# One output-weight chunk loaded early, experts and combine in one block, the inverses' transpose moved: a two-layer trunk on one core

## What is computed

```python
for layer in range(2):
    mix = hybrid_mixer(h, ...) if layer == 0 else rglru_mixer(h, ...)   # both end in @ w_out
    h = layer_norm(DN_ALPHA * h + mix, ln_g[layer, 0], ln_b[layer, 0])
    ffn = hierarchical_moe(h, ...)          # top group, then top 2 of its 8 experts
    h = layer_norm(DN_ALPHA * h + ffn, ln_g[layer, 1], ln_b[layer, 1])

# in hybrid_mixer, per chunk and head
t_inv = triangular_solve(eye + lower, eye, lower=True, unit_diagonal=True)
# in hierarchical_moe, per block of 128 rows of one expert
hid = silu(xi @ w_gate[e]) * (xi @ w_up[e]); yb = hid @ w_down[e]
y = segment_sum(yb * row_w[:, None], row_tok)
```

## Time and profile before

| | us |
|---|---|
| median of three runs | 2292.05 |
| lowest, highest | 2288.58, 2295.93 |
| the profiled execution's own time | 2292.08 |
| its span | 2290.3 |

### The profile page before, as it was taken

The page is one execution under the profiler, slowest core; times in us unless marked ns, Lnnn a source line. Parts: engine busy times, 40 slices in busy tenths (PEclk is TensorE's granted clock), DMA queues, the critical chain, the costliest instruction groups (busy, mean ns, idle before and its releaser), DMA issues. The chain is left out here.

```text
span 2290.3 us, 30226 instructions
## 1 busy us (share of the span) xinstructions
PE 2137.8 (93%) x10785; PEld 1741.7 (76%) x10785; DVE 1746.2 (76%) x1785; ACT 1409.3 (62%) x1509; POOL 499.4 (22%) x325
## 2 busy tenths in 40 slices
PE   8999966989999999999997999999899999999985
PEld 7777755878688888888883777768688888888862
DVE  5378866563799899889985785564799888988867
ACT  3344445253278877888775438753377888788852
POOL 0000040001223333333320001111133333333322
PEclk9999978999899999999998899999899999999997
DMA  4121011140199999999974231060299999999955
GB/s 157 47 66 45 28 30 56 25 196 38 43 359 391 381 385 386 399 387 393 386 267 174 89 114 37 19 241 37 99 365 395 381 384 397 383 397 385 391 199 239
DMA packets 133823, 526.12 MB, mean 230 GB/s; under 512 B 36816, under 2 KB 41328, under 8 KB 99952
## 3 DMA queue, kind: packets, MB, share of 16 engines
q1 hardware_dynamic: 114736, 491.46, 56.6%
q0 software_dynamic: 19008, 33.60, 3.9%
HBM read 505.32 MB, written 51.92 MB: 243 GB/s over the span
## 5 line engine op out<-in xcount | busy, mean ns | idle before, releaser
L2284 DVE TENSOR_TENSOR w_lo_e<-raw,w_hi_e 128x2048 fp32r<-128x2048 f32 x192 | 439.3, 2293 | 55.3 <-ACT w_hi_e L2236 50.3
L2236 ACT ACTIVATE w_hi_e<-raw 128x2048 fp32r<-128x2048 f32 x192 | 367.7, 1918 | 127.4 <-PE ps L1481 103.8
L1479 PE MATMUL ps<-w_hi_e,x_hi_e 128*128 128x512 f32 x1024 | 407.8, 398 | 6.0 <-DVE x_lo_e L2289 5.3
L1481 PE MATMUL ps<-w_hi_e,x_lo_e 128*128 128x512 f32 x1024 | 401.1, 392 | 0.0
L1480 PE MATMUL ps<-w_lo_e,x_hi_e 128*128 128x512 f32 x1024 | 400.9, 391 | 0.0
L2284 DVE TENSOR_TENSOR w_lo_e<-raw_more_e,w_hi_e 128x2048 fp32r<-128x2048 f32 x128 | 292.9, 2288 | 49.5 <-ACT w_hi_e L2236 49.4
L2236 ACT ACTIVATE w_hi_e<-raw_more_e 128x2048 fp32r<-128x2048 f32 x128 | 245.7, 1919 | 17.7 <-PE ps L1481 14.9
L2144 POOL DMA_INDIRECT expert_rows<-hT,idx_e x64 | 98.1, 1533 | 669.3 <-ACT hT L2250 669.3
L1479 PEld LDWEIGHTS ps<-w_hi_e,x_hi_e 128*128 128x128 f32 x1024 | 193.6, 189 | 45.4 <-DVE x_lo_e L2289 5.7
L1481 PEld LDWEIGHTS ps<-w_hi_e,x_lo_e 128*128 128x128 f32 x1024 | 193.4, 189 | 41.5
L1480 PEld LDWEIGHTS ps<-w_lo_e,x_hi_e 128*128 128x128 f32 x1024 | 193.8, 189 | 38.0
(11 more groups left out here) (441 smaller groups left out, 4337.6 us busy)
## 6 DMA issues: line engine op xcount, KB each, us to landing
raw<-in_moe_w_up SPq DMA_DIRECT2D x126, 1024.0 KB, 7.8
raw_more_e<-in_moe_w_down SPq DMA_DIRECT2D x64, 1024.0 KB, 7.7
raw_more_e<-in_moe_w_gate SPq DMA_DIRECT2D x62, 1024.0 KB, 7.1
hT<-in_moe_w_gate SPq DMA_DIRECT2D x62, 1024.0 KB, 7.0
raw<-in_moe_w_down SPq DMA_DIRECT2D x62, 1024.0 KB, 8.9
y_c<-expert_rows SPq DMA_DIRECT2D x32, 512.0 KB, 11.0
h_rows<-h SPq DMA_DIRECT2D x24, 512.0 KB, 3.4
w_ch<-in_w_ch SPq DMA_DIRECT2D x17, 512.0 KB, 3.6
```

Source lines behind the costliest of these rows:

```text
L1479: pe.matmul(out, lhs[0], rhs[0], start=start, stop=False)
L1481: return pe.matmul(out, lhs[1], rhs[0], start=False, stop=stop)
L2236: act.activation(w_hi[:, p.split, :], ring[p.raw], ACT.Copy).then_inc(taken, 1)
L2284: v.tensor_tensor(w_lo[:, p.split, :], ring[p.raw], w_hi[:, p.split, :].bitcast(F32), ALU.subtract).then_inc(split, 1)
```

## The change

It has three parts.

1. `inverse.turn` goes, in ScalarE's loop over attention's tiles, from behind `copy_share(6)` to ahead of `exps(7)`.
2. `combine` has no block of its own any more. It returns five functions that `expert_blocks` calls at the end of each engine's queue, in its own block. In the place of the barrier stand a semaphore `rows_there`, which GpSimd raises after its last wait for the scatters and SyncE waits for before the first load of y_c, and TensorE's wait for the last split of gathered rows. TensorE's idle matmuls go from 2 on PSUM bank 7 to 6 on bank 5. The tile y_c now lies over tiles of the experts.
3. In layer 1, chunk 6 of w_out is loaded in the recurrent block, when its weight buffer is free, and SyncE waits for it at the end of that block. `mix_and_route` loads the other seven, takes chunk 6 first, and has the order y0, w0, y1, w1. TensorE's idle matmuls at its start go from 5 to 3. The tiles of w_out and of the recurrent weights have fixed places for this.

```diff
+        at_out = at_end - 4 * KC * D
+        w_last = tuple(nc.alloc_sbuf_tensor_at(x, [P, KC, D], dt, offset=at_out) for x, dt in (("w_out_last", F32), ("w_out_last_r", F32R)))
+        place = at_end - 4 * 2 * KC * P
+        w_ch = tuple(nc.alloc_sbuf_tensor_at(x, [P, 2, KC, P], dt, offset=place) for x, dt in (("rw_ch", F32), ("rw_ch_r", F32R)))
...
-                    recurrent(m, gate, gate_r, w_ch)
+                recurrent(m, gate, gate_r, w_ch, w_last[0][:, EARLY_CHUNK, :])
...
-                expert_blocks(m, layer, raw, landed, route)
-            if layer == 0:
-                w_ch = sb_both("rw_ch", [P, 2, KC, P], scope=first)
-            combine(m, layer, out if layer == 1 else None, w_ch[0])
+                expert_blocks(m, layer, raw, landed, route, out if layer == 1 else None, w_ch[0])
...
@@ attention, scalar
                 for t in range(NT + 1):
+                    if t == NT - 1:
+                        inverse.turn(act)
                     if t < NT:
                         exps(t)
                     if t:
                         copy_p(t - 1)
                         copy_share(t - 1)
-                    if t == NT - 1:
-                        inverse.turn(act)
@@ recurrent, sync
+                sp.wait_ge(proj, N - 1)
+                sp.dma_start(w_early, a["w_out"][1][:, EARLY_CHUNK, :]).then_inc(s_early, 16)
+                sp.wait_ge(s_early, 16)
@@ mix_and_route
-        there = KC // 2 if half_there else 0
+        chunk = [EARLY_CHUNK] + [c for c in range(KC) if c != EARLY_CHUNK] if layer else list(range(KC))
+        there = 1 if layer else KC // 2
...
-        order = [("y", 0), ("y", 1), ("w", 0), ("w", 1), ("y", 2), ("w", 2), ("w", 3), ("y", 3),
+        order = [("y", 0), ("w", 0), ("y", 1), ("w", 1), ("y", 2), ("w", 2), ("w", 3), ("y", 3),
...
-                    sp.dma_start(w_out[:, n, :], a["w_out"][layer][:, n, :]).then_inc(s_w[n], 16)
+                    sp.dma_start(w_out[:, chunk[n], :], a["w_out"][layer][:, chunk[n], :]).then_inc(s_w[n], 16)
...
-                idle(m, pe, 7, 2 if half_there else 5)
+                idle(m, pe, 7, 3 if layer else 2)
@@ expert_blocks: sync, gpsimd, tensor, scalar, vector
+                transfer(sp)
...
+                pool.sem_inc(rows_there, 1)
+                add_shift(pool)
...
+                pe.wait_ge(x_split, 2 * r + 3)
+                mix_and_turn(pe)
...
+                root_and_evict(act)
...
+                normalise(v)
@@ combine
+    def transfer(sp):
+        sp.wait_ge(rows_there, 1)
         rows = m.y_dram.rearrange("(k t p) d -> t k p d", k=2, p=P)
...
-                idle(m, pe, 7, 2)
+        idle(m, pe, 5, 6)
```

More of the change, by code:

```diff
@@ L2030, in expert_blocks @@
     with scope:
+        with ExitStack() as passing:
+            y_c = sb(n_("y_c"), [P, NT, 2, D], scope=passing)
         more = sb(n_("raw_more"), [P, RAW - EARLY - 1, PIECE], scope=scope)
@@ new lines, in combine, with add_shift @@
+    gained, ready, last_ready, turned, copied, high_out, stored, s_dve = (sem(n_(x)) for x in
+        ("gained", "ready", "last_ready", "turned", "ht_out", "high_out", "stored", "dve"))
+    LAST = NT - 1
+    span = lambda t: slice(t * P, (t + 1) * P)
+    half = lambda hf: slice(hf * HALF, (hf + 1) * HALF)
+    def add_shift(pool):
+        if last:
+            pool.wait_ge(s_ln, 16)
+            for t in range(LAST):
+                pool.wait_ge(gained, t + 1)
+                pool.tensor_tensor(h[:, t, :], h[:, t, :], ln[:, 1, :], ALU.add).then_inc(ready, 1)
@@ new lines, in mix_and_turn, with mix, turn @@
+    def mix_and_turn(pe):
+        def mix(t):
+            pe.wait_ge(spread, t + 1)
+            for hf in range(2):
+                if t >= 2:
+                    pe.wait_ge(summed, 2 * (t - 2) + hf + 1)
+                for k in range(2):
+                    if hf == 0:
+                        pe.wait_ge(s_y[t][k], 16)
+                    mm = pe.matmul(ps[:, 2 * (t % 2) + hf, :], diag[:, t, k, :], y[:, t, k, half(hf)],
+                                   start=(k == 0), stop=(k == 1))
+                mm.then_inc(mixed, 1)
+        def turn(t):
+            pe.wait_ge(normed, t + 1)
+            if t == LAST:
+                pe.wait_ge(high_normed, 1)
+            if t >= 2:
+                pe.wait_ge(copied, t - 1)
+            for c in range(KC):
+                mm = pe.transpose(ps[:, 4 + 2 * (t % 2) + c // 4, (c % 4) * P:(c % 4 + 1) * P], h[:, t, c::KC], m.c(C_ID))
+            mm.then_inc(turned, 1)
+        idle(m, pe, 5, 6)
+        for t in range(NT):
+            mix(t)
+            if t >= 2 and not last:
+                turn(t - 2)
+        if not last:
+            turn(LAST - 1)
+            turn(LAST)
```

279 lines of the change are left out of this document (118 added, 161 removed).

## The result

The changed kernel takes **2276.28 us** (median of six executions, 2274.72 to 2277.67), the kernel before 2294.32 in the same comparison (2288.58 to 2298.59): ratio 0.993, 95% interval 0.9912 to 0.9949, so 12 to 20 us less. The forecast was 2276.2. Run once more as an experiment the changed kernel took 2278.6, ratio 0.9937 (0.9923 to 0.995).

What follows compares the result with a forecast made beforehand. TensorE, busy 93% of the span, was taken to lose time at joints between stages where one other queue works alone. Terms -4.5 - 11.3 + 1.1 - 1.2 = -15.9 took 2292.05 to 2276.2 us, range 2271.5 to 2284.

Steps and rivals of the forecast that it cites:

- part 1, attention: End of attention: transposes, their store and the 16 loads run earlier, SyncE ending at 389.85 for 394.33; -4.5 us.
- delta rule's clock: Start of the delta rule's stage: a shorter TensorE gap might change the half-clock stretch; between -1.2 and +1.0, taken as 0.
- part 2, first load of y_c, per layer: Experts to combine: SyncE's first load follows GpSimd's wait without its drain; -5.65 us per layer, -11.3 together.
- clock in the combine, layer 0: Start of layer 0's combine: a short fall to half clock after a 3.7 us TensorE gap; costs 0.8 us.
- clock in the combine, layer 1: Start of layer 1's combine: short clock fall mostly covered by TensorE's wait for tile 1's rows; costs 0.3 us.
- part 3 at the stage's end: Layer 1's projection: VectorE's 1.23 us wait is filled, later splits come 1.2 us earlier; -1.2 us in the sum.
- attention's last VectorE instruction ends at 387.04 + 2.0: End of attention: VectorE's tail moves 2.0 us later to 389.1, still 0.8 us before SyncE ends.
- The drain is over 5.5 us after that load at the latest.: Layer 1's combine: GpSimd's drain ends within 5.5 us of the first load, before its first addition some 9 us after.
- with half of the fall inside the gap: Layer 0's combine: half the clock's fall passes while TensorE is idle, so it costs 0.8 us in place of 2.3.
- long fall: Rival, both combines: half clock lasts 10 us from about the first product; +5.5 in place of +1.1, 2280.6 us; chance 0.14.
- The first product later than 6.5 us after the first load: Sign against the prediction, in the combine: a first product that late after the first load of y_c would prove it wrong.
- Another stage has changed its length by over 1 us: Sign against the prediction: any stage outside the change differing by over 1 us would prove it wrong.

Runs made afterwards that it cites:

- idle10: Changed kernel with ten idle matmuls in place of six ahead of each combine; 2275.64 us.
- gains_second: Changed kernel with ten idle matmuls ahead of each combine and layer 1's gains and shifts loaded behind tile 1's rows; 2271.4 us, ratio 0.9904.
- all_three: Changed kernel with ten idle matmuls, the gains behind tile 1's rows, and rank(0) moved two chunks into the last tile's products; 2270.44 us, ratio 0.9901.
- three_late_chunk: all_three with part 3 undone (no early chunk, order y0, y1, w0, w1, five idle matmuls); 2272.64 us, ratio 0.9917.
- after: The changed kernel itself, in its first measurement and profile, against the kernel before; 2276.28 us, ratio 0.993.
- after_again: The changed kernel run once more with no edit; 2278.6 us, ratio 0.9937.
- halves: Changed kernel with the two 512 KB loads of tile 0's rows split by columns into four of 256 KB, low halves first; 2281.43 us.
- turn_back: Changed kernel with only part 1 undone, the transposes behind tile 6's copies again; 2280.39 us, ratio 0.9949.
- late_chunk: Changed kernel with only part 3 undone: all eight chunks loaded at layer 1's projection, order y0, y1, w0, w1, five idle matmuls; 2275.61 us, ratio 0.9921.
- rank_apart: Changed kernel with rank(0)'s narrow matmuls moved two chunks into the last tile's products, in both layers; 2277.14 us.
- drain_first: Changed kernel with a GpSimd drain added between its last scatter wait and the raise of rows_there, each expert stage; 2287.24 us, ratio 0.9978.

## Why the prediction was right, point by point

The time was right to 0.1 us, which is partly luck. The forecast was 15.9 us less than 2292.05; the kernel before, measured again beside the changed one, took 2294.32, and the medians differ by 18.0. The terms measured in the first pair of profiles add up to -18.2 (-4.21 - 5.87 + 0.88 - 1.21 - 5.88 - 1.94) where the sum had -15.9, and scatter in the rest gives 0.8 back.

| term | forecast | measured |
|---|---|---|
| part 1, attention | -4.5 | -4.2 |
| delta rule's clock | 0 | -1.4 in one profile, scatter of 4.4 |
| part 2, first load of y_c, per layer | -5.65 | -5.9 |
| clock in the combine, layer 0 | +0.8 | +0.9; over the five kernels with six idle matmuls, whole loads and no added drain +0.9 to +2.4 |
| clock in the combine, layer 1 | +0.3 | -1.9; -0.8 to -1.9 |
| part 3 at the first addition | -1.2 | -1.2 |
| part 3 at the stage's end | -1.2 | +0.1 to -0.3 |

**Part 1.** The step "attention's last VectorE instruction ends at 387.04 + 2.0" was short by 1.2. The 2.0 of the moved instruction were right. But TensorE now pauses 3.3 us while ScalarE has the transposes and tile 7's exponentials, and its clock is down from 381.8 to 385.2, when the tail comes. Timeline of TensorE, turning the exponentials of tiles 6 and 7, in the changed kernel:

```profile
376.09 1.09 PE L626 MATMUL ps<-cst,scores 128*128 128x128 f32 x8
...
383.12 1.97 PE L626 MATMUL ps<-cst,scores 128*128 128x128 f32 x8
```

and before:

```profile
382.92 1.09 PE L627 MATMUL ps<-cst,scores 128*128 128x128 f32 x8
```

Tile 7's eight take 1.97 us in place of 1.09. So the margin of 0.8 us became -0.5, and the term 4.2 in place of 4.5. The profiles of idle10 and gains_second, whose code is the same here, bear the cause out: no stretch at half clock begins there, tile 7's eight take 1.09 us, and attention's last VectorE operation ends 58.6 and 58.7 us after the barrier in place of 60.1, ahead of SyncE, as forecast.

**Part 2.** The reading of the queue was right in both its halves, that the raise does not wait for the drain and that the drain alone was the hold: the first load stands 0.02 us behind the wait, and a drain put ahead of the raise costs 5.5 us again. The Trainium skill's rule on increments and drains (PSUM — Partial Sum Buffer, Engine vs sequencer instructions) agrees with both rows. One sentence failed: "The drain is over 5.5 us after that load at the latest." In layer 1 the drain stands behind GpSimd's last addition, 42 us after that load, and is what the closing barrier waits for last. In the eleven profiles with the joined block and no added drain that barrier opens 0.37 us behind SyncE's drain, in the other three 0.16. So the forecast left out 0.2 us, and whoever shortens the stores at the kernel's end will meet GpSimd's drain first.

**The clock in the combine.** The sign was wrong in layer 1, and with it that of the whole term: +1.1 forecast, -1.1 measured. Two steps failed. First, "with half of the fall inside the gap": in the changed kernel hardly any of it was, 0.2 us of 3.4 in layer 0 and 0.4 in layer 1. In the six profiles with six idle matmuls, one block and no drain, the fall in layer 0 begins 2.9 to 4.4 us after the first load, from 0.9 us ahead of the first product to 0.7 behind it. In layer 0 the profiles then fall into three groups:

| stretch at half clock, layer 0 | kernels | combine, us |
|---|---|---|
| none | gains_second, all_three, three_late_chunk, idle10 | 47.8, 47.8, 47.8, 48.5 |
| 3.4 us | after, after_again, halves | 49.1, 49.2, 49.2 |
| 6.8 us, from 2.9 to 3.0 on | turn_back, late_chunk, rank_apart | 50.4, 50.5, 50.5 |

Against the three at 47.8 the fall costs 1.3 to 1.5 or 2.6 to 2.8 us, and which of the two differs between executions. Why idle10 takes 0.7 more without a fall, from tile 1 on, no run says. The second group is the forecast's, the third lies toward the rival "long fall", to which I gave 0.14; it was there in three of six. Second, for layer 1 I compared only tile 0. The earlier trace rows show that TensorE waits 2.07 us for tile 1's rows, and I counted that as cover. I did not see that the wait itself lets the clock fall a second time: the record behind it takes 4.12 us for five matmuls, 0.82 each, which is the half-clock figure that I had used for tile 0. With the wait gone (gains_second, all_three, three_late_chunk) this fall is gone; yet the wait of 2.46 us in halves had none. The change took it away by making tile 0 slower. The advice in the Trainium skill against idle gaps (TensorE: Matmul & The Clock Gate, Why this matters for your kernels) was right about the mechanism in layer 0, where filling the gap takes the fall away; in layer 1 filling that gap alone made the combine longer, since another gap came behind it.

**Part 3.** Right at the place where it was derived, the first addition, and wrong in carrying it to the sum. "The later splits come 1.2 us earlier" holds through to the last addition; the stage's end does not follow, in both pairs of kernels.

**The signs that I named.** The first load behind the wait by under 0.5 us, the order of the transposes, and no idle time ahead of the first chunk: all there. Of the signs against, two were there as well. "The first product later than 6.5 us after the first load" came true with 7.29, and was badly put, since my own term of 0.8 implies 6.9. "Another stage has changed its length by over 1 us" came true for four (the first projection -2.1, the delta rule -1.4, layer 1's routing +1.9, and its experts up to the end of GpSimd's wait +1.6); this was scatter, and I had no measure of it from one profile. Layer 1's projection and routing shows how it arises. In the eleven profiles with rank(0) in its old place it takes 140.7 to 140.8 us four times, 143.6 to 143.8 five times, and 142.4 and 143.0 once each. In the first group a stretch at half clock of 3.4 us begins 105.6 to 105.8 us after the barrier; in the second one of 6.8 us at 105.3 to 105.4 (105.7 in late_chunk, where all of it is 1.2 later), and 3.4 us more at half clock follow before the stage ends (from 125.8 or 125.9 on; in late_chunk the last stretch begins 3 us sooner).

## What to carry to other kernels

The barrier here cost what its slowest drain took, which stands in the rows of the queue instructions on the block's own line: look there first, above all at GpSimd where it has issued indirect transfers, and let a semaphore stand for the barrier if one can. Then look where the drain has gone: here it moved to the kernel's end and binds there by 0.2 us. A wait that looks like cover for a slow engine must also be asked what it does to the clock of the one that waits, and filling a gap pays only where no other follows: ten idle matmuls alone lost in layer 1 what they gained in layer 0, while with the gains' load moved as well both combines became shorter, by 1.3 to 2.8 and 1.5 to 2.7 us. One profile of each kernel cannot tell a stage's change from scatter of 2 to 4 us; the stage's length over several kernels that leave it alone can.

## What the runs showed of the hardware

- GpSimd's first drain behind a stage of indirect transfers takes 5.46 us with nothing else pending and 7.86 behind an addition of 2.34; a second drain takes 0.03 and 2.45. The 5.4 us are paid once, even 42 us after the last transfer has landed. GpSimd's drains in the blocks without indirect transfers take 0.03 to 0.3 us with nothing pending.
- A pause of TensorE of 3.7 us ahead of the combine was followed by a stretch at half clock of 3.4 or 6.8 us, one of 7.1 us by 6.8, one of 9.2 us (drain_first) by 10.2, and one of 0.3 us by none. Behind shorter waits it went either way: 2.07 and 2.19 us with a fall, 2.46 (halves) without. Between executions of like code the start moves by up to 1.5 us, and with it the length between the two values. In layer 1's projection and routing, 6.8 us more at half clock went with 3.0 us more time (143.7 for 140.7).
- A stretch at half clock also began with TensorE busy for 4.69 of the 4.90 us before it (after_again), the last 3.4 us of them on narrow matmuls (16 of 128x36 and 20 of 128x32). In layer 1 it did so in eleven profiles of eleven; with wide products put between the two kinds it did not begin there, in three of three.
- TensorE started 3.4 and 3.7 us after the issue of a first load of 256 KB, and 3.7 and 3.8 us after one of 512 KB: the size hardly matters there.
